# The last step of a convolutional FFN layer's down projection: row tiles of 1024 columns finished whole, or in two halves of 512

## What is computed

```
x = x + rmsnorm(merged @ w_out, norm_mix_post)
# channel mixing
f = rmsnorm(x, norm_ffn_pre) @ w_up          # 1024 -> 2 * 2816
f = causal_dwconv(f, ffn_conv_w, ffn_conv_b) # width 3
gate, val = split(f, 2)
f = (gelu(gate) * val) @ w_down              # 2816 -> 1024
x = x + rmsnorm(f, norm_ffn_post)
# rmsnorm(y, g) = y * rsqrt(mean(y * y) + 1e-6) * g
```

## Time and profile before

| | us |
|---|---|
| median of 3 runs (816.42 to 917.29) | 820.07 |
| the profiled execution, its own time | 818.04 |
| span of the slowest core in it (core 7), first to last instruction | 816.5 |
| spans of all 8 cores in it | 803.0 to 816.5 |
| TensorE busy on core 7 | 722.2 (88%) |
| VectorE, ScalarE, GpSimd busy | 485.1, 392.8, 276.3 |

### The profile page before, as it was taken

How to read it: one execution, slowest core, us unless ns; L and a number is a source line. 1 busy time by engine, 2 the same in 40 slices (tenths; PEclk the granted TensorE clock), 3 DMA queues, 4 the chain that set the end, 5 groups by cost and what they waited for, 6 DMA issues and landing times.

```text
span 816.5 us, 10998 instructions; the slowest of 8 cores (803.0 to 816.5 us)
## 1 busy us (share of the span) xinstructions
PE 722.2 (88%) x3636; PEld 327.1 (40%) x3636; DVE 485.1 (59%) x563; ACT 392.8 (48%) x537; POOL 276.3 (34%) x284
## 2 busy tenths in 40 slices
PE   4886966887888997987899899999999999999995
PEld 1332423343334442433444344444444444444442
DVE  1804679773895488655567676222578877772222
ACT  3156687568635864737655454110344554441111
POOL 3114233552362265542354444000134444331000
PEclk9898977999798998999999999999999999999998
DMA  8975003260444142997379644132444444401221
GB/s 172 172 225 204 1 1 104 52 155 0 78 104 104 27 78 36 146 171 186 56 130 245 141 78 78 64 140 85 135 92 69 85 75 76 81 5 46 110 104 77
DMA packets 23959, 81.47 MB, mean 100 GB/s; under 512 B 2912, under 2 KB 3424, under 8 KB 23904
## 3 DMA queue, kind: packets, MB, share of 16 engines
q0 software_dynamic: 12672, 41.20, 30.0%
q1 hardware_dynamic: 11232, 39.58, 14.0%
HBM read 96.78 MB, written 16.78 MB: 139 GB/s over the span
## 4 chain that ended last, share of the span: by engine, by line
PE 61%; DMA 12%; DVE 10%; issue 7%; ACT 5%; POOL 3%; DVEq 0%; SPq 0%; POOLq 0%; ACTq 0%
PE ps L605 60%; DMA ye<-x 6%; DMA xT<-xT 3%; DMA out<-ye 2%; DVE xc L585 2%; DMA wc<-w_in_r 2%; DVE hT L585 2%; PE ps L609 1%; DVE tv L585 1%; POOL st L581 1%; ACT tg L576 1%; POOL a L581 1%; DVE thx L851 1%; ACT L576 1%; DVE tg L585 1%
## 5 line engine op out<-in xcount | busy, mean ns | idle before, releaser
L605 PE MATMUL ps<-h2T,wu 128*128 128x512 bf16 x1408 | 314.7, 384 | 21.0 <-DVE tg L585 10.0
L605 PEld LDWEIGHTS ps<-h2T,wu 128*128 128x128 bf16 x1408 | 137.0, 98 | 189.5 <-issue 31.6
L605 PE MATMUL ps<-wdn,u 128*128 128x512 bf16 x704 | 152.3, 379 | 0.0
L581 POOL TENSOR_TENSOR u<-tg,tv 128x1024 bf16<-128x1024 f32 x44 | 104.5, 2375 | 125.2 <-DVE tv L581 68.7
L585 DVE SCALAR_TENSOR_TENSOR tg<-ps,pp,tg 128x1023 f32<-128x1023 f32 x88 | 112.6, 1280 | 39.1 <-ACT tg L576 28.3
L585 DVE SCALAR_TENSOR_TENSOR tv<-ps,pp,tv 128x1023 f32<-128x1023 f32 x88 | 112.6, 1280 | 29.4 <-ACT tv L576 15.0
L605 PE MATMUL ps<-hT,wc 128*128 128x512 bf16 x416 | 108.0, 414 | 19.9 <-DVE hT L585 10.2
L605 PEld LDWEIGHTS ps<-wdn,u 128*128 128x128 bf16 x704 | 68.7, 98 | 83.3
L585 DVE SCALAR_TENSOR_TENSOR yf<-ps,st,g 128x1024 f32<-128x1024 f32 x16 | 20.5, 1284 | 110.2 <-POOL st L581 70.3
L576 ACT ACTIVATE yf<-ps 128x1024 f32<-128x1024 f32 x16 | 16.4, 1023 | 129.4 <-PE ps L605 129.4
L591 POOL TENSOR_SCALAR st<-st 128x1 f32<-128x1 f32 x48 | 17.1, 356 | 178.0 <-ACT yf L576 127.7
(11 more groups left out here) (99 smaller groups left out, 694.4 us busy)
## 6 DMA issues: line engine op xcount, KB each, us to landing
wu<-w_up_r POOLq DMA_DIRECT2D x44, 512.0 KB, 5.6
xT<-xT SPq DMA_DIRECT2D x16, 512.0 KB, 6.0
ye<-x POOLq DMA_DIRECT2D x16, 512.0 KB, 7.0
out<-ye SPq DMA_DIRECT2D x16, 512.0 KB, 4.8
xf<-out SPq DMA_DIRECT2D x16, 512.0 KB, 3.3
out<-xf SPq DMA_DIRECT2D x16, 512.0 KB, 2.7
wdn<-w_down_r POOLq DMA_DIRECT2D x11, 512.0 KB, 9.6
ye<-w_out_r SPq DMA_DIRECT2D x8, 512.0 KB, 6.9
```

The lines of the kernel that those rows point to most:

```text
L581: return P.op(eng, lambda e: e.tensor_tensor(out=AP_(out), in0=AP_(in0), in1=AP_(in1), op=op), reads, writes, dur)
L605: return (lambda e: e.matmul(AP_(out), lhsT=lhsT, rhs=rhs, start=start, stop=stop), tuple(reads), tuple(writes), max(n / 2400.0 + 0.003, 0 ...
```

## The change

In `f_down` the end of a row tile is done in two halves of 512 columns, in another order. Squares: one for each half, into a scratch tile `yq` in bfloat16, each with its own sum. VectorE multiplies each half of `y` by the norm's weight into `yf` without waiting for the row factor. GpSimd adds epsilon to the first half's sum, then adds the second half's sum, then raises to the power -0.5: three small instructions in place of two. VectorE makes one multiply-add for each half, `yf` times the row factor plus x, and SyncE stores each half by a DMA of its own.

```diff
     def g_bufs():
         P.dma("sp", g2[:, 0, :], gbc_d[:, 2, :], 524288, writes=[g2.k(0)], slot=("g2", 0))
         F_["xf"] = [A.alloc("xf", [128, D], F32) for _ in range(3)]
+        F_["yq"] = A.alloc("yq", [128, 512], BF16)
         F_["yf"] = [A.alloc("yf", [128, D], F32) for _ in range(2)]
...
-        P.dma("sp", xb[:], out_d[tsl, :], 524288, reads=[("out", t)], writes=[xb.k()], slot=("xf", t % 3))
+        yq = F_["yq"]
+        P.dma("sp", xb[:], out_d[tsl, :], 524288, reads=[("out", t)], writes=[xb.k(), xb.k(0), xb.k(1)], slot=("xf", t % 3))
...
-        m1, r1 = stat(1), stat(1)
-        act(yy[:], y.flat(), AF.Square, y.keys(), [st.k("n1", t), yy.k()], 1024, scale=1.0 / 32, accum=sv(m1))
-        rsqrt(r1, m1, 1, [st.k("n1", t)], st.k("nr", t))
-        stt(yy[:], y.flat(), sv(r1), g2[:, 0, :], ALU.mult, ALU.mult, y.keys() + [st.k("nr", t), g2.k(0)], [yy.k()], 1024)
-        tt("dve", xb[:], xb[:], yy[:], ALU.add, [xb.k(), yy.k()], [xb.k()], 1024)
-        P.dma("sp", out_d[tsl, :], xb[:], 524288, reads=[xb.k()], writes=[("out", t)], slot=("xoo", t % 3))
+        m1, r1 = stat(2), stat(1)
+        for dh in range(2):
+            hs = slice(dh * 512, (dh + 1) * 512)
+            act(yq[:], y.flat(dh, 1), AF.Square, y.keys(dh, 1), [st.k("n1", t, dh), yq.k()], 512, scale=1.0 / 32,
+                accum=sv(m1 + dh))
+            tt("dve", yy[:, hs], y.flat(dh, 1), g2[:, 0, hs], ALU.mult, y.keys(dh, 1) + [g2.k(0)], [yy.k(dh)], 512)
+        ts("pool", sv(m1), sv(m1), EPS, 1.0, ALU.add, ALU.mult, [st.k("n1", t, 0)], [st.k("n1", t, 0)], 1)
+        ts("pool", sv(r1), sv(m1), sv(m1 + 1), 1.0, ALU.add, ALU.mult, [st.k("n1", t, 0), st.k("n1", t, 1)],
+           [st.k("nre", t)], 1)
+        tt("pool", sv(r1), sv(r1), cpw[:, 0:1], ALU.pow, [st.k("nre", t)] + CPW, [st.k("nr", t)], 100)
+        for dh in range(2):
+            hs = slice(dh * 512, (dh + 1) * 512)
+            stt(xb[:, hs], yy[:, hs], sv(r1), xb[:, hs], ALU.mult, ALU.add, [yy.k(dh), st.k("nr", t), xb.k()],
+                [xb.k(dh)], 512)
+            P.dma("sp", out_d[tsl, hs], xb[:, hs], 262144, reads=[xb.k(dh)], writes=[("out", t, dh)], slot=("xoo", t % 3, dh))
```

## The result

The changed kernel takes 828.0 us (median of 4 runs, 827.03 to 828.19) where the kernel before, in 4 runs, has 818.71. The ratio is 1.0121 [1.009, 1.0151]: slower by 1.2%. The forecast was 815.0 us, the wrong side of no change. The forecast's own range of 808 to 822 us misses the result; the wide range of 804 to 829 holds it. Some runs are disturbed and some per cent longer, and comparisons leave them out, which is why a median can belong to a longer list of times than its ratio.

What follows compares the result with a forecast made beforehand. The time was taken as TensorE's matmuls, plus gaps of the first 461 us, plus a bare 9.7 us end. Forecast: 818.04 - 2.1 (end) - 0.9 (tables) = 815.0 us; own range 808 to 822, wide range 804 to 829.

Steps and rivals of the forecast that it cites:

- the new plan: Planner's redrawn order of the first 461 us: 0.9 us gained from table loads, 7 us allowed to either side.
- the end of the last tile: Bare end after the last matmul: square 0.42, multiply-adds 1.1, stores 0.65, less 0.1 for waits; gain 2.1 us (0.8 to 3.0).
- My own bound for "wrong": Sign of a wrong forecast: gaps of TensorE's first stretch differing from 84.5 us by more than 7.
- The tables: ScalarE changes function sets 28 times in place of 32; four fewer loads gain 0.9 us (0 to 5.1).
- GpSimd. [...] Gain 0: Last tile: two GpSimd instructions still follow the second square (0.19 and 0.55 us), the third is done early; gain 0.
- The store: Last tile's half store, half the bytes, lands at 1.95 us in place of 2.6: gain 0.65 us (0 to 1.3).
- my own list: Signs of a wrong forecast, among them multiply-adds of 0.9 us and a landing of 2.6 us for half the bytes.
- The other 15 tiles: Earlier row tiles: VectorE's added 6 us and 16 more stores hide under TensorE's matmuls; cost 0, without slack 6 us.
- Rival D: Added VectorE work not hidden at the joints between down and up projection: 6 us, 821 us; chance 0.05.
- A: Rival: the program's end does not shorten, only the tables' 0.9 us is gained: 817.1 us; chance 0.12.
- B: Rival: attention's weighted sums wait for their Exp, TensorE's 13.6 us of PT waits double: 828.6 us; chance 0.19.
- C: Rival: the new plan closes gaps, hT and tg waits lose a third, 9.2 us: 805.8 us; chance 0.14.

Runs made afterwards that it cites:

- the draws: Planner's random start set to 2, 3, 4 (old and new tile ends) and 5 (new), against 1 in both kernels: nine orders, 816.83 to 828.0 us.
- start 1: Planner's random start left at 1: the kernel before (old tile ends) 818.71 us, the changed kernel (new tile ends) 828.0 us, ratio 1.0121.
- start 4: Planner's random start set to 4 in place of 1: old tile ends 821.78 us (ratio 1.0026), new tile ends 818.38 us (1.0003).

## Why the prediction was wrong in sign

Two steps of the prediction failed. The first sets the sign: the new plan was put at -0.9 us, from the table loads alone, with 7 us to either side, and the runs put it at +9 (827.22 us for the old code in the new order). The second is the end of the last tile: 2.1 us were forecast and 0.22 came, since GpSimd's closing DRAIN, which the sum does not have, ended the program.

**The new plan: a term that I had mis-sized.** "For the gaps as a whole I have no directed term", with 7 us to either side. The order was the whole effect: 1.0113 without any of the new code. The allowance was derived from what timing does to one order from core to core, 13.5 us, halved. What another order does was not in any row, and the draws show it directly: 9 us between the two of start 1 on the median, and 11 us on the mean of all cores over all compared runs (811.3 and 822.6 us). My own bound for "wrong" (gaps differing from 84.5 us by more than 7) is just not reached at 91.2, since 2.5 us of the loss came as slower matmuls, which the gaps don't count: 0.91 against 0.92 of the clock over 380 us.

**The tables.** "Four fewer are 5.1 us of ScalarE, and at five in thirty 0.9 us of the time." The count was near (27 where about 26 were expected), the worth was not to be seen: three loads fewer in the slowest order of nine. A share of the chain read from one order does not price the same instruction in another.

**The end of the last tile.** The arithmetic held and the sum did not. VectorE's and ScalarE's part came out at 1.63 us for 1.52 forecast (0.42 and 1.1), the stretch from the issue of the last store to SyncE's closing at 0.48 (2.95 to 2.47 us) for 0.55. The multiply hidden beside GpSimd is hidden, the multiply-adds have the 0.75 us that I took between 0.68 and 0.92, and the squares the 0.60; the gap of 0.06 us between the multiply-adds, taken without a row, is an overlap of 0.08. What failed is the step "GpSimd. [...] Gain 0", and its silent companion that SyncE's last wait ends the program. Nothing in the earlier trace rows says so: from the landing of the last store to the end of the span there was a rest that I attributed to closing work without reading the rows of the closing line. They would have shown that GpSimd, not SyncE, was last, by 1.3 us. So only the part of the gain that also moves GpSimd's last power counts: the shorter square, 0.42, less 0.08 for a GpSimd instruction that takes 0.27 us where it took 0.19, and 0.12 by which ScalarE and GpSimd start later behind what releases them. That leaves the 0.22 measured.

**The store.** In the changed kernel 2.6 us became 2.1, a gain of 0.5 where the row gave 0.65. That is not firm: in the new code in the old order the last half took 2.9 to 3.0 us on all eight cores, more than the whole store before, which by my own list was a sign of being wrong. What sets a half's landing is open. The Trainium skill (DMA: Bandwidth & Descriptors, section "Anatomy of one DMA") gives its 2.0 us plus the bytes at 436 GB/s for a DMA that GpSimd issues; these stores are SyncE's. By that rate, as an estimate, halving 512 KB brings 0.6 us and not the 0.3 of the prediction, which took the page's 2.0 off the measured 2.6. The traces do not show the 2.0 for SyncE's stores: 1.3 us beside the bytes of the whole store, and some 1.4 to 1.5 beside those of the half.

**The other 15 tiles.** "Cost 0" is shown twice: the equal 303.7 us of the down projections and the up projection between them, and the ratio 1.0002. Rival D (6 us, 821) falls with it.

**The rivals.** A (the end does not shorten) had the right outcome through another mechanism: neither the store nor VectorE was fixed, something else was last. B gave 828.6 us, and 828.0 was measured, but not for its reason: that the two agree, and that the wide range holds the result by B's price, is luck. TensorE's waits for PT rose from 13.6 to 18.2 us, not to 27.2, and more was lost at `gl` (4.9) and `at` (5.8); nor does it belong to the changed kernel, since with start 4 the new form shows 13.4 us and takes 818.4. C (the order closes gaps) had the right place and the wrong sign in this draw. That hT and tg lose a third came true (27.5 to 18.2 us) while the time rose: in this pair waits of one group were exchanged for others, and one group did not tell the sum. The 16 us that the prediction took as the least that a measurement can tell from no change were too coarse: the ratio's interval is 0.6% wide and excludes 1. Its chances, too, were given for 802 to 834 us, not for the range of 804 to 829.

**What stays open.** Which positions in the first 460 us make one order 10 us better than another was not tested; the loss is spread over every stage of it, and no single wait in either trace is larger than 8 us. Nor was any order chosen by measuring many of them; among these nine none was clearly faster than the kernel before.

## What to carry to other kernels

Where a search with a random part sets the order of a program, any edit redraws it: measure the edit in the old order and the old code in the new order before the edit is judged, and count the spread of a few draws (here 11 us, 1.3%) as the uncertainty of every single comparison of two orders. Ahead of any work on a kernel's end, read which queue issues the last instruction. Here it was GpSimd's, and making the last row factor on ScalarE in its place shortened the end by 1.7 us by itself and let the halves bring their 2.0.

## What the runs showed of the hardware

The closing DRAIN of GpSimd's queue took 7.857 to 7.862 us on every core of every trace, with TensorE busy beside it or idle, and its row began 0.03 us ahead of GpSimd's last instruction: at 808.4 us in the kernel before, at 798.7 where its last work had been moved away. Those of the other engines took 4.08 us (TensorE, over 0.05 us behind its last matmul), 0.007 us (SyncE), 0.2 to 1.1 (ScalarE) and 1.0 to 1.4 (VectorE). So this program does not end earlier than 7.9 us after the start of GpSimd's last instruction. That instruction was the same small power of 0.55 us in every run, so whether the DRAIN has the same length behind another one is not shown.

One program on eight cores with equal work gives spans from 803.0 to 816.5 us in one execution of the kernel before and from 820.2 to 826.6 in one of the changed kernel. The spread is one of executions more than of orders: over the compared runs it is 5.8 to 12.2 us in 24 of the kernel before and 6.4 to 10.1 in 4 of the changed one.
